# Where a mixer's adaptive-norm terms are summed, turned and loaded, on one core

## Chip, cores, metric

The kernel runs on one core of a Trainium2 chip. The metric is the time of one launch on the device in microseconds (us). Five engines matter: TensorE (PE; its weight loads are shown apart as PEld), VectorE (DVE), ScalarE (ACT), GpSimd (POOL), and SyncE (SP), whose queue issues nearly all loads from HBM.

## What is computed

Two layers of a trunk over 256 latent tokens and 256 context tokens, width 1024, all in float32. Each layer has three sublayers: a feed-forward block, a token mixer, a feed-forward block. Each sublayer's input is modulated and its output gated by terms computed from a conditioning vector (one for each of the two streams):

```python
mods_x = jnp.split((silu(c) @ ada_w[l] + ada_b[l])[:, None, :], 9, axis=-1)
x = ffn_sublayer(x, mods_x[0:3], ...)          # shift, scale, gate
y_x, y_c = token_mixer(modulate(x, sh_x, sc_x), modulate(ctx, sh_c, sc_c), ...)
# end of the mixer:
y_x = (sigmoid(g_ret)*y_ret + sigmoid(g_na)*y_na + sigmoid(g_fou)*y_fou) @ w_o
x = layer_norm(ALPHA * x + g_x * y_x, ln_w[l, 1], ln_b[l, 1])
x = ffn_sublayer(x, mods_x[6:9], ...)
```

In layer 1 the context stream ends with the keys and values of the mixer, so from there on only 256 tokens are left.

## The kernel before

**Sublayers.** `i` counts them from 0 to 5; the mixers are i = 1 (layer l = 0, both streams in the merge, N = 512 columns) and i = 4 (l = 1, one stream, N = 256). The order of every engine's work is written out by hand.

**Weights** come in units of 512 KB through a ring of 4 buffers: SP's `unit` (L389) loads `raw`, ACT's `rounded` (L517) writes the high part `wh`, DVE's `split` (L875) the low part `wl`, and PE multiplies three times for each pair of operands (`three`, L1360 to L1362). SP loads unit u when DVE has split unit u-4; ACT rounds unit u when PE has finished unit u-4. SP issues strictly in program order: a load that waits holds up all loads behind it.

**Adaptive-norm terms.** While a mixer or feed-forward block runs, DVE forms the sums for the next one (`ada`, L887 for the first term, L890 for the others): each step takes 128 rows of `ada_w` from one of only two buffers `araw` (SP's `ada_load`, L397) and adds them, scaled, to `acc`, one accumulator for each stream. The load of step n waits until step n-2 is done. A mixer has 24 steps: 8 for its own gate, 8 for the next shift (w = 0), 8 for the next scale (w = 1). Each finished sum is turned by eight 128x128 transposes into two PSUM banks (PE `mixer_turn`, L1421) and summed from there by DVE (`mixer_mods`, reduce L934, in bulk 1.2 us, and a small add L939). `acc` may be written again only after the turn.

**The merge** is the stage in question. Eight rounds `mm` = 0 to 7, each of five units: `v` (gate of branch 0), `v+1`, `v+2`, `v+3` (two half products), `v+4`; they use PSUM banks 0 to 5 (7 for the first product of all). After a round, DVE does `MERGE_PACE[mm]` steps of `ada`; between `v+3` and `v+4` of round mm, SP issues `MERGE_LOADS[mm]` loads. Ten steps are done ahead of the merge, 14 inside it. Before the change both layers share one pace, 2 2 2 0 3 3 2 0, and one table of loads, 0 2 2 2 2 3 2 1. In rounds 3 and 7 PE turns stream 0's sum between `v+2` and `v+3`, into banks 6 and 7; in layer 0 it turns stream 1's after `v+4` (into 2 and 3 for w = 1).

**The output projection** (`down`, matrix `w_o`) follows, in units q of its own: 8 in layer 1; 16 in layer 0, where the first 8 work on tiles 0 and 1 and the others on tiles 2 and 3. Its tiles take the banks `OUT_BANKS`: (6,7), (0,1), (2,3), (4,5) in layer 0, (6,7) and (0,1) in layer 1. Its moving operand is staged by ACT (L552) and DVE (L1029); the first four stages are done at the end of round 7, behind the rounding and splitting of that round's last unit. Before its first product PE also waits until stream 0's scale has been read out of banks 6 and 7 (`mod_taken`), and at q = 8 until the terms are ready (`mods_ready`).

Of the kernel before, what the change touches and what calls it, by code (L numbers as in the profile page):

```python
# [30 lines left out]
KD = D // P  # L31
# [86 lines left out]
def trunk(nc, io, out):  # L118
# [3 lines left out]
    with ctx:  # L122
# [140 lines left out]
        def both(i):  # L263

            return tiles(i) == NT
# [14 lines left out]

        def mod_bank(w, st):

            return 2 if w and st else 6

        def free_bank(i, n):

# [71 lines left out]
            return 1 + gate_halves(i) + 2 * sum(mod_sums(j) for j in range(i))  # L358

        MERGE_ADA = KD + 2  # L360
        MERGE_PACE = (2, 2, 2, 0, 3, 3, 2, 0)
        MERGE_LOADS = (0, 2, 2, 2, 2, 3, 2, 1)

        ada_ops = list(itertools.accumulate((chunk_streams(s, w) for i in range(-1, SUBS) for s, w in chunks(i) for _ in range(KD)),
                                            initial=0))
# [14 lines left out]
        def _(sp):  # L380
# [70 lines left out]
            def mixer(l):  # L451
                i = 3 * l + 1
                win = io["mix_w_in"][l]
                u = AT["ret_in", l]
                for n, (r, lo, hi) in enumerate(ret_steps(l)):
                    c0 = C_RG if r < KD else C_RK - KD * P if r < 12 else C_RQ - 12 * P
                    unit(u + n, rows(win, c0 + r * P, P))
                for k in range(KD):
                    unit(AT["rv", l] + k, rows(win, C_RV, D, k, k + 1))
                for j in range(4):  # L460
                    unit(AT["fu", l] + j, rows(win, C_FU + j * P, P))
                gate_bias(i)
                u = AT["na_in", l]
                for n in range(AR):
                    ada_load(i, n)
                for gi, c0 in enumerate((C_NK, C_NQ)):
                    for j in range(4):
                        unit(u + 4 * gi + j, rows(win, c0 + j * P, P))
                for j in range(4):
                    unit(AT["nv", l] + j, rows(win, C_NV, 512, 2 * j, 2 * j + 2))  # L470
                    if j:
                        ada_load(i, AR + j - 1)
                for n in range(AR + 3, MERGE_ADA):
                    ada_load(i, n)
                for h in range(4, NH):

                    sp.wait_ge(n_max, n0[l] + len(n_items[l]) // 4 * (h // 2 - 2) + 3 + h % 2)
                    load_bias(sp, l, h)
                u = AT["merge", l]
                for mm in range(KD):  # L480
                    c = mm * P
                    v = u + 5 * mm
                    unit(v, rows(win, c + C_GT, P))
                    unit(v + 1, rows(io["ret_w_out"][l], c, P))
                    unit(v + 2, rows(win, c + (C_GT + D), P))

                    unit(v + 3, rows(io["na_fou_w_out"][l], c, P))
                    for n in range(MERGE_LOADS[mm]):
                        ada_load(i, MERGE_ADA + sum(MERGE_LOADS[:mm]) + n)
                    unit(v + 4, rows(win, c + (C_GT + 2 * D), P))  # L490
                for q in range(KD * (2 if both(i) else 1)):
                    unit(AT["wo", l] + q, rows(io["mix_w_o"][l], 0, D, q % KD, q % KD + 1))
                    if q == KD - 2:
                        ln_params(i)
# [361 lines left out]
        def _(dve):  # L856
# [175 lines left out]
            def down(i, u, src, n):  # L1032

                for q in range(TAIL, n * (2 if both(i) else 1)):
                    split(u + q)
                    stage(i, src, n, q)
                    if both(i):
                        k0 = q - n
                        if k0 == 4:
                            residual(i + 1, 0)  # L1040
                        if k0 == (6 if n == KF else 5):
                            residual(i + 1, 1)
                        if k0 == (8 if n == KF else 6):
                            front(i + 1, 0)
                        if k0 == (10 if n == KF else 7):
                            front(i + 1, 1)
                        if k0 == 16:
                            rest(i + 1, 0)
                        if k0 == 18:
                            rest(i + 1, 1)  # L1050
# [164 lines left out]
            def mixer(l):  # L1215
# [74 lines left out]
                for mm in range(KD):  # L1290
                    v, q = u + 5 * mm, 5 + 40 * l + 5 * mm
                    z = rgz[:, mm, 0:N]

                    def gated(w, out, bank, uu):
                        dve.wait_ge(g_sig, 3 + 24 * l + 3 * mm + w + 1)
                        dve.wait_ge(unit_done, v + uu)
                        V.tensor_tensor(out, sg[:, w, 0:N], ps[:, bank, 0:N], ALU.mult).then_inc(g_sum, 1)

                    split(v + 4)
                    split(v + 5)  # L1300
                    gated(0, z, 1, 2)
                    split(v + 6)
                    split(v + 7)
                    for n, (w, bank) in enumerate(((1, 3), (2, 4))):
                        if n:
                            split(v + 8)
                            if mm == KD - 1:
                                for t in range(TAIL):
                                    stage(i, rgz, KD, t)
                        gated(w, sg[:, w, 0:N], bank, 4)  # L1310
                        dve.wait_ge(g_sum, q + 2 + 2 * n)
                        V.tensor_tensor(z, z, sg[:, w, 0:N], ALU.add).then_inc(g_sum, 1)
                        dve.wait_ge(g_sum, q + 3 + 2 * n)
                        if n == 0 and mm in (3, 7):
                            mixer_mods(i, mm // 4, 0)
                    if mm in (3, 7) and htiles(i + 1) == NT:
                        mixer_mods(i, mm // 4, 1)
                    for n in range(MERGE_PACE[mm]):
                        ada(i, MERGE_ADA + sum(MERGE_PACE[:mm]) + n)
                down(i, AT["wo", l], rgz, KD)  # L1320

            dve.sem_inc(ff_mul, 2)
# [32 lines left out]
        def _(pe):  # L1355
# [76 lines left out]
            def down(i, u, n):  # L1432
# [15 lines left out]

                if i % 3 == 1:
                    pe.wait_ge(g_sum, 5 + 40 * l + 5 * (KD - 1) + 1)  # L1450
                    pe.wait_ge(mod_taken, 4 * l + htiles(i + 1) // LT + 1)
                total = 2 * n if both(i) else n
                for q in range(total - TAIL):
                    half, k0 = divmod(q, n)
                    staged(q)
                    if q == n:
                        if i % 3 == 1:
                            pe.wait_ge(g_sum, 5 + 40 * (l + 1))
                            pe.wait_ge(mods_ready, 2 * (i + 2))
                        else:  # L1460
                            pe.wait_ge(ff_mul, 2 + ff0(i) + len(ffn_steps(i)))
                    if n == KF and half:
                        if k0 == 10:
                            turn(i + 1, 0)
                        if k0 == 12:
                            turn(i + 1, 1)
                    for t in range(LT * half, LT * half + LT):
                        ins = product(q, t, first=k0 == 0, last=k0 == n - 1)
                    ins.then_inc(unit_done, 1)
# [195 lines left out]
            def mixer(l):  # L1665
# [85 lines left out]
                for mm in range(KD):  # L1751
                    v, sgn, smn = u + 5 * mm, 24 * l + 3 * mm, 40 * l + 5 * mm

                    pe.wait_ge(g_sig, sgn + 1)
                    if mm:
                        form_a(v, 0, src, N)
                    pe.wait_ge(g_sum, smn + 1)
                    form_a(v + 1, 1, (oh, ol), N, src_at={0: (o_lo, 3 * l + 1), 4: (o_lo, 3 * l + 2), 6: (o_lo, 3 * l + 3)} if mm == 0 else {})
                    pe.wait_ge(g_sig, sgn + 2)
                    form_a(v + 2, 2, src, N)  # L1760
                    if mm in (3, 7):
                        mixer_turn(i, mm // 4, 0)
                    pe.wait_ge(g_sum, smn + 4)
                    if mm == 0:
                        pe.wait_ge(n_lo, 4 * (l + 1))
                    form_a(v + 3, 3, (ah, al), N, kts=4, last=False)
                    form_a(v + 3, 4, (fh, fl), N, kts=4, row=4)
                    pe.wait_ge(g_sig, sgn + 3)
                    form_a(v + 4, 5, src, N)
                    if mm in (3, 7) and htiles(i + 1) == NT:  # L1770
                        if mm == 7:
                            pe.wait_ge(g_sig, sgn + 5)
                            pe.wait_ge(g_sum, smn + 7)
                        mixer_turn(i, mm // 4, 1)
                down(i, AT["wo", l], KD)

            pe.wait_ge(c_silu, 1)
# [83 lines left out]
```

## Time and profile before

| | us |
|---|---|
| three runs | 2497.81, 2503.41, 2503.57; median 2503.41 |
| the profiled execution | 2500.18 |
| its span, first to last instruction | 2498.4 |
| busy PE / PEld / DVE / ACT / POOL | 2383.4 / 2080.4 / 1602.4 / 949.7 / 140.6 |

What is busy says little by itself: PE is, nearly always. What counts is where PE idles or runs at a lower clock, who releases it there, and what that engine had waited for in turn. In the rows below a line of a timeline reads: start, duration, engine, line of the kernel, operation, output tile <- inputs, shape, count, and in brackets the idle time before it with the releaser. SPq is SP's queue of DMA issues. A timeline merges equal neighbours: `x3` with 5.00 us is three issues with what lay between them.

### The profile page before, as it was taken

Reading aid. Unit: us, or ns where it says so; the run is one execution under the profiler, and the core shown is the slowest. Engines: PE = TensorE matmul, PEld = TensorE weight load, DVE = VectorE, ACT = ScalarE, POOL = GpSimd, SP = SyncE. Lnnn points to the kernel's source line nnn. Section 1 sums busy time; section 2 is a strip of 40 time slices with the busy share of each in tenths; the row PEclk is TensorE's granted clock in tenths of the full one; section 3 lists DMA queues with packets and bytes.
Section 4 is the critical chain, followed back from the end, with each engine's and each line's share of the span. In section 5 each row is a group of like instructions: output and inputs, shape, how many; then the busy total and the mean of one; then the engine's idle time right before and its main releaser. Section 6 shows DMA issues by size and latency. Waiting matters only on the chain.

```text
span 2498.4 us, 33234 instructions
## 1 busy us (share of the span) xinstructions
PE 2383.4 (95%) x13346; PEld 2080.4 (83%) x13346; DVE 1602.4 (64%) x2094; ACT 949.7 (38%) x1407; POOL 140.6 (6%) x171
## 2 busy tenths in 40 slices
PE   6999999999999999979999999999999999976997
PEld 6888988998877888778889898889888887975996
DVE  5566658856377446676666786666786647755655
ACT  2522345442136222353224463224564225333443
POOL 2000001101100000020000110000010110001000
PEclk8999999999999999989999999999999999987999
DMA  8445555652232425545456575456565334664763
GB/s 271 136 161 176 193 192 171 177 179 65 54 108 82 150 91 169 168 126 161 154 175 199 172 219 169 152 169 202 177 186 167 97 118 127 203 213 135 225 203 118
DMA packets 476669, 400.53 MB, mean 160 GB/s; under 512 B 36324, under 2 KB 428644, under 8 KB 476260
## 3 DMA queue, kind: packets, MB, share of 16 engines
q1 hardware_dynamic: 460640, 390.13, 49.2%
q10 hardware_dynamic: 15876, 8.28, 1.1%
q8 instruction: 106, 1.74, 0.3%
q14 instruction: 47, 0.39, 0.0%
HBM read 397.19 MB, written 1.17 MB: 159 GB/s over the span
## 4 chain that ended last, share of the span: by engine, by line
PE 84%; DVE 8%; ACT 3%; issue 2%; DMA 2%; ACTq 1%; POOL 0%; SPq 0%; POOLq 0%; DVEq 0%
PE ps L1360 25%; PE ps L1362 25%; PE ps L1361 25%; DVE wl L875 2%; PE ps L1571 1%; ACT wh L517 1%; ACT tB L535 1%; PE ps L1387 1%; PE ps L1649 1%; DVE st L943 1%; PE ps L1737 1%; PE ps L1628 1%; PE ps L1394 1%; DMA raw<-in_mix_w_in 1%; DVE nms L1185 1%
## 5 line engine op out<-in xcount | busy, mean ns | idle before, releaser
L875 DVE TENSOR_TENSOR wl<-raw,wh 128x1024 fp32r<-128x1024 f32 x576 | 701.6, 1221 | 651.9 <-ACT wh L517 650.5
L517 ACT ACTIVATE wh<-raw 128x1024 fp32r<-128x1024 f32 x576 | 609.1, 1059 | 1268.0 <-PE ps L1362 1166.0
L1360 PE MATMUL ps<-hh,wh 128*128 128x256 f32 (+1 forms) x2736 | 898.7, 328 | 44.3 <-DVE hl L976 19.8
L1361 PE MATMUL ps<-hl,wh 128*128 128x256 f32 (+1 forms) x2736 | 890.1, 325 | 0.0
L1362 PE MATMUL ps<-hh,wl 128*128 128x256 f32 (+1 forms) x2736 | 889.8, 325 | 0.0
L1360 PEld LDWEIGHTS ps<-hh,wh 128*128 128x128 f32 x2736 | 526.6, 192 | 90.5 <-issue 22.9
L1361 PEld LDWEIGHTS ps<-hl,wh 128*128 128x128 f32 x2736 | 526.5, 192 | 41.6 <-issue 1.0
L1362 PEld LDWEIGHTS ps<-hh,wl 128*128 128x128 f32 x2736 | 526.2, 192 | 40.6
L890 DVE SCALAR_TENSOR_TENSOR acc<-araw,c,acc 128x1024 f32<-128x1024 f32 x210 | 258.4, 1279 | 47.0 <-DMA araw<-in_ada_w 45.6
L1360 PE MATMUL ps<-wh,stage_h_f 128*128 128x512 f32 x616 | 240.8, 391 | 2.0 <-DVE stage_l_f L1029 2.0
L1362 PE MATMUL ps<-wh,stage_l_f 128*128 128x512 f32 x616 | 239.8, 389 | 0.0
L1361 PE MATMUL ps<-wl,stage_h_f 128*128 128x512 f32 x616 | 239.8, 389 | 0.0
L807 POOL TENSOR_SCALAR mv<-mv 128x1 f32<-128x1 f32 x42 | 41.5, 988 | 1868.5 <-DVE mv L945 1868.5
L1360 PEld LDWEIGHTS ps<-wh,stage_h_f 128*128 128x128 f32 x616 | 115.7, 188 | 27.6 <-DVE wl L875 4.3
L1362 PEld LDWEIGHTS ps<-wh,stage_l_f 128*128 128x128 f32 x616 | 115.6, 188 | 24.4
L1361 PEld LDWEIGHTS ps<-wl,stage_h_f 128*128 128x128 f32 x616 | 115.7, 188 | 23.7
L1360 PE MATMUL ps<-wh,hh 128*128 128x512 f32 x192 | 77.1, 402 | 2.4 <-DVE wl L875 2.2
L1361 PE MATMUL ps<-wl,hh 128*128 128x512 f32 x192 | 75.5, 393 | 0.0
L1362 PE MATMUL ps<-wh,hl 128*128 128x512 f32 x192 | 75.3, 392 | 0.0
L1029 DVE TENSOR_TENSOR stage_l_f<-g,stage_h_f 128x256 fp32r<-128x256 f32 x154 | 64.4, 418 | 0.0
L535 ACT ACTIVATE tB<-ps,modT 128x128 f32<-128x128 f32 x176 | 63.4, 465 | 1.1 <-PE ps L1429 1.1
L552 ACT ACTIVATE stage_h_f<-g 128x256 fp32r<-128x256 f32 x154 | 61.6, 400 | 0.0
(164 smaller groups left out, 2292.5 us busy)
## 6 DMA issues: line engine op xcount, KB each, us to landing
raw<-in_ffa_w SPq DMA_DIRECT2D x204, 512.0 KB, 3.8
raw<-in_ffb_w SPq DMA_DIRECT2D x168, 512.0 KB, 4.0
raw<-in_mix_w_in SPq DMA_DIRECT2D x148, 512.0 KB, 4.0
araw<-in_ada_w SPq DMA_DIRECT2D x136, 512.0 KB, 4.9
raw<-in_mix_w_o SPq DMA_DIRECT2D x24, 512.0 KB, 4.2
raw<-in_ret_w_out SPq DMA_DIRECT2D x16, 512.0 KB, 4.8
raw<-in_na_fou_w_out SPq DMA_DIRECT2D x16, 512.0 KB, 4.1
raw<-in_ada_w SPq DMA_DIRECT2D x8, 512.0 KB, 5.0
```

The lines of the kernel that those rows point to most:

```text
L517: A.activation(wh[:, s, :], raw[:, s, :], ACT.Copy).then_inc(w_rounded, 1)
L535: ins = A.activation(tB[:, t % 2, k * P:(k + 1) * P], y[:, k], ACT.Identity, scale=modT[:, i % 2, 1, k, s:s + 1], bias=modT[:, i % 2, 0, k ...
L552: A.activation(sh_[:, q % TAIL], src[:, k0, half * SEQ:(half + 1) * SEQ], ACT.Copy).then_inc(stage_hi, 1)
L807: link(G.tensor_scalar(m[:, 1:2], m[:, 1:2], EPS, None, ALU.add))
L875: V.tensor_tensor(wl[:, s, :], raw[:, s, :], f(wh[:, s, :]), ALU.subtract).then_inc(w_split, 1)
L890: ins = V.scalar_tensor_tensor(out=acc[:, st], in0=araw[:, m % AR], scalar=c, in1=acc[:, st], op0=ALU.mult, op1=ALU.add)
L943: ins = V.bn_stats(st[:, which, t % 2, 6 * k:6 * k + 6], src[:, k * 512:(k + 1) * 512])
L1029: V.tensor_tensor(sl_[:, q % TAIL], src[:, k0, half * SEQ:(half + 1) * SEQ], f(sh_[:, q % TAIL]), ALU.subtract).then_inc(stage_lo, 1)
L1185: link(V.tensor_reduce(nmax[:, t % 3, 0:1], y[:, 0:key_n(items[t])], AXX, ALU.max))
L1360: T.matmul(out, a[0], b[0], start=start, stop=False)
L1361: T.matmul(out, a[0], b[1], start=False, stop=False)
L1362: return T.matmul(out, a[1], b[0], start=False, stop=stop)
```

## The change

It has four parts, all in the two mixers. (1) `mod_bank`: the scale (w = 1) is turned into banks 2 and 3 for both streams, the shift into 6 and 7. (2) The turn of the scale's stream 0 moves from between `v+2` and `v+3` of round 7 to behind the last unit of the merge, with waits for the readers of banks 2 and 3; DVE sums it after its last `g_sum` addition, and PE's wait for `mod_taken` before the projection goes. (3) In layer 0, the turn of the scale's stream 1 moves from the end of the merge into the projection, before the products of q = 4; DVE sums it after its stage q = 6. (4) Layer 1 gets a pace and a table of loads of its own: pace 2 2 2 2 2 2 2 0, loads 0 2 2 2 2 2 2 2. Layer 0's stay.

```diff
         def mod_bank(w, st):
-            return 2 if w and st else 6
+            return 2 if w else 6
-        MERGE_PACE = (2, 2, 2, 0, 3, 3, 2, 0)
-        MERGE_LOADS = (0, 2, 2, 2, 2, 3, 2, 1)
+        MERGE_PACE = ((2, 2, 2, 0, 3, 3, 2, 0), (2, 2, 2, 2, 2, 2, 2, 0))
+        MERGE_LOADS = ((0, 2, 2, 2, 2, 3, 2, 1), (0, 2, 2, 2, 2, 2, 2, 2))
 # DVE, down
                     stage(i, src, n, q)
+                    if n == KD and both(i) and q == 6:
+                        mixer_mods(i, 1, 1)
 # DVE, merge
-                        if n == 0 and mm in (3, 7):
-                            mixer_mods(i, mm // 4, 0)
-                    if mm in (3, 7) and htiles(i + 1) == NT:
-                        mixer_mods(i, mm // 4, 1)
-                    for n in range(MERGE_PACE[mm]):
+                        if n == 0 and mm == 3:
+                            mixer_mods(i, 0, 0)
+                    if mm == 3 and htiles(i + 1) == NT:
+                        mixer_mods(i, 0, 1)
+                    if mm == 7:
+                        mixer_mods(i, 1, 0)
+                    for n in range(MERGE_PACE[l][mm]):
 # PE, down
                     pe.wait_ge(g_sum, 5 + 40 * l + 5 * (KD - 1) + 1)
-                    pe.wait_ge(mod_taken, 4 * l + htiles(i + 1) // LT + 1)
...
+                    if n == KD and both(i) and q == 4:
+                        mixer_turn(i, 1, 1)
 # PE, merge
-                    if mm in (3, 7):
-                        mixer_turn(i, mm // 4, 0)
+                    if mm == 3:
+                        mixer_turn(i, 0, 0)
...
-                    if mm in (3, 7) and htiles(i + 1) == NT:
-                        if mm == 7:
-                            pe.wait_ge(g_sig, sgn + 5)
-                            pe.wait_ge(g_sum, smn + 7)
-                        mixer_turn(i, mm // 4, 1)
+                    if mm == 3 and htiles(i + 1) == NT:
+                        mixer_turn(i, 0, 1)
+                pe.wait_ge(g_sig, 24 * l + 3 * (KD - 1) + 5)
+                pe.wait_ge(g_sum, 40 * l + 5 * (KD - 1) + 7)
+                mixer_turn(i, 1, 0)
                 down(i, AT["wo", l], KD)
```

## Rows read from the trace of the kernel before

**Rows 1.** The page's first part: busy time, share of the span, instructions.
```profile
PE 2383.4 (95%) x13346; PEld 2080.4 (83%) x13346; DVE 1602.4 (64%) x2094; ACT 949.7 (38%) x1407; POOL 140.6 (6%) x171
```

**Rows 2.** Busy time by stretch, layer 1's merge: length, engines, PEclk, DMA share, GB/s.
```profile
2130.00:2144.40 14.40, 14.40 (x123) 14.40 (x122) 10.37 (x13) 6.11 (x8) 0.00 (x0) 1.00 0.82 256
...
2174.00:2188.40 14.40, 14.40 (x122) 14.40 (x121) 8.29 (x12) 3.72 (x5) 0.00 (x0) 1.00 0.21 62
2188.40:2206.00 17.60, 11.44 (x77) 11.27 (x76) 7.92 (x9) 6.10 (x8) 0.00 (x0) 0.81 0.67 201
2206.00:2226.00 20.00, 15.68 (x115) 15.51 (x114) 10.80 (x13) 5.24 (x7) 0.00 (x0) 0.83 0.79 234
```

**Rows 3.** Timeline of PE, layer 1's merge: both turns and both stalls.
```profile
2159.50 1.04 PE L1421 MATMUL ps<-ident,acc 128*128 128x128 f32 x8
2160.29 0.36 PE L1360 MATMUL ps<-ah,wh 128*128 128x256 f32 x1
2160.49 0.28 PE L1361 MATMUL ps<-al,wh 128*128 128x256 f32 x1
...
2198.36 0.55 PE L1360 MATMUL ps<-hh,wh 128*128 128x256 f32 x1 [6.16 <-DVE wl L875]
...
2219.59 0.55 PE L1360 MATMUL ps<-hh,wh 128*128 128x256 f32 x1 [4.32 <-DVE wl L875]
...
2233.14 1.03 PE L1421 MATMUL ps<-ident,acc 128*128 128x128 f32 x8
```

**Rows 4.** Timeline of ACT, layer 1's merge: the rounding that ends the first stall.
```profile
2195.90 1.06 ACT L517 ACTIVATE wh<-raw 128x1024 fp32r<-128x1024 f32 x1 [13.79 <-DMA raw<-in_mix_w_in]
```

**Rows 5.** Timeline of SP's queue, layer 1's merge: when loads are issued.
```profile
2144.18 1.05 SPq L397 DMA_DIRECT2D araw<-in_ada_w  x2
...
2158.58 1.05 SPq L397 DMA_DIRECT2D araw<-in_ada_w  x2
...
2171.68 0.37 SPq L389 DMA_DIRECT2D raw<-in_na_fou_w_out  x1
2184.78 5.00 SPq L397 DMA_DIRECT2D araw<-in_ada_w  x3
```

**Rows 6.** Timeline of DVE, layer 1's merge: steps of the sums in rounds 2 and 4.
```profile
2154.33 2.67 DVE L890 SCALAR_TENSOR_TENSOR acc<-araw,c,acc 128x1024 f32<-128x1024 f32 x2
...
2184.00 0.75 DVE L887 TENSOR_SCALAR acc<-araw,c 128x1024 f32<-128x1024 f32 x1
```

**Rows 7.** Timelines of PE, ACT and DVE at the ends of both merges.
```profile
1019.46 1.03 PE L1421 MATMUL ps<-ident,acc 128*128 128x128 f32 x8
1022.52 0.73 PE L1360 MATMUL ps<-wh,stage_h_m 128*128 128x512 f32 x1 [2.02 <-DVE stage_l_m L1029]
...
2243.33 0.47 PE L1360 MATMUL ps<-wh,stage_h_m 128*128 128x512 f32 x1 [3.41 <-DVE stage_l_m L1029]
...
1019.72 1.06 ACT L517 ACTIVATE wh<-raw 128x1024 fp32r<-128x1024 f32 x1 [4.38 <-PE ps L1362]
...
2240.02 1.06 ACT L517 ACTIVATE wh<-raw 128x1024 fp32r<-128x1024 f32 x1 [1.81 <-PE ps L1362]
...
1020.81 1.22 DVE L875 TENSOR_TENSOR wl<-raw,wh 128x1024 fp32r<-128x1024 f32 x1 [1.63 <-ACT wh L517]
...
2240.29 1.22 DVE L934 TENSOR_REDUCE modT<-ps 128x8 f32<-128x1024 f32 x1
...
2241.63 1.22 DVE L875 TENSOR_TENSOR wl<-raw,wh 128x1024 fp32r<-128x1024 f32 x1
```

**Rows 8.** Busy time by stretch at both ends: columns as in rows 2.
```profile
2240.00:2250.00 10.00, 6.67 (x22) 5.37 (x23) 5.86 (x11) 3.91 (x8) 0.00 (x0) 0.83 0.51 153
1020.00:1030.00 10.00, 7.98 (x31) 6.30 (x30) 6.82 (x11) 3.90 (x9) 0.00 (x0) 0.83 0.40 124
```

**Rows 9.** Timelines of DVE and ACT, layer 0's projection: what surrounds the moved turn.
```profile
1024.74 1.22 DVE L934 TENSOR_REDUCE modT<-ps 128x8 f32<-128x1024 f32 x1
...
1035.39 1.06 ACT L517 ACTIVATE wh<-raw 128x1024 fp32r<-128x1024 f32 x1 [1.35 <-PE ps L1362]
...
1036.48 1.23 DVE L875 TENSOR_TENSOR wl<-raw,wh 128x1024 fp32r<-128x1024 f32 x1 [1.16 <-ACT wh L517]
```

More of the change, by code:

```diff
@@ L487, in mixer @@
                     unit(v + 3, rows(io["na_fou_w_out"][l], c, P))
-                    for n in range(MERGE_LOADS[mm]):
-                        ada_load(i, MERGE_ADA + sum(MERGE_LOADS[:mm]) + n)
+                    for n in range(MERGE_LOADS[l][mm]):
+                        ada_load(i, MERGE_ADA + sum(MERGE_LOADS[l][:mm]) + n)
                     unit(v + 4, rows(win, c + (C_GT + 2 * D), P))
@@ L1313, in mixer @@
                         dve.wait_ge(g_sum, q + 3 + 2 * n)
-                        if n == 0 and mm in (3, 7):
-                            mixer_mods(i, mm // 4, 0)
-                    if mm in (3, 7) and htiles(i + 1) == NT:
-                        mixer_mods(i, mm // 4, 1)
-                    for n in range(MERGE_PACE[mm]):
-                        ada(i, MERGE_ADA + sum(MERGE_PACE[:mm]) + n)
+                        if n == 0 and mm == 3:
[5 more added lines that the diff above has]
+                    for n in range(MERGE_PACE[l][mm]):
+                        ada(i, MERGE_ADA + sum(MERGE_PACE[l][:mm]) + n)
                 down(i, AT["wo", l], rgz, KD)
```

## The prediction

> **What bounds the kernel now.** I read the page's busy times first: PE is busy for 2383.4 of 2498.4 us [rows 1], so anything that keeps PE neither idle nor at a lower clock is free, and a change can win only in the 115 us of idle time and in the stretches of low clock beside them. The change touches the two merges and the projections behind them, so I cut these into stretches. In layer 0's merge PE has no idle time between rounds; each unit is 24 products of 512 columns there. In layer 1's it is at full load and full clock in rounds 1 to 4, and then 17.6 and 20.0 us long stretches show it busy for only 11.44 and 15.68 us, with a clock of 0.81 and 0.83 [rows 2]. So layer 1's rounds 5 and 6 hold most of what can be had.
>
> PE's timeline names the stalls: 6.16 and 4.32 us, both ended by a split of weights on DVE [rows 3]. The rest follows by asking each releaser what it had waited for. The split waited for ACT's rounding, and that had stood idle for 13.79 us for a load of `raw` [rows 4]. Was the transfer slow or late? SP's queue answers: its last weight issue ends at 2171.68 + 0.37 = 2172.05 and the next issue of anything is at 2184.78, 12.7 us later, and it is a load of `araw` [rows 5]. In the stretch of 2174 to 2188 the DMA engines move 62 GB/s, against 256 before [rows 2]: they had nothing to do. The `araw` load waited for the step two before it, number 16, and DVE ran that at 2184.00 to 2184.75 [rows 6], 0.03 us before the issue. Step 16 is the first of round 4, since round 3 has a pace of 0; the load that needs it is put in SP's round 5, which SP reaches a round ahead of DVE. The second stall is the same pattern one round later. Layer 0 has the same tables, but the four units in the ring are twice as long there, and PE does not see the pause.
>
> **Part 1, the new pace in layer 1.** It removes no work: 14 steps and 14 loads before and after. Step 16 moves to the end of round 3 and the three-step rounds are gone. The cost of the stall is read from the two turns on PE, which stand in the same place of rounds 3 and 7: 2233.14 - 2159.50 = 73.64 us [rows 3]. Four undisturbed rounds take 4 x 14.40, the pitch of the `araw` loads [rows 5] and the length of the stretch with PE at 14.40 [rows 2]: 57.60. The turn of round 3 lies between too. It is 0.79 us to the next product, and that product keeps 0.20 instead of 0.12 us to its follower [rows 3]: 0.87. So 73.64 - 57.60 - 0.87 = **15.2 us** are lost. Of these 6.16 + 4.32 = 10.5 are idle, and the other 4.7 are mainly the products at about half the clock behind each stall (it falls after 6.16 and 4.32 us without work).
>
> Does all of it go? What decides is which comes last before an `araw` load. With an even pace the two steps that a pair of loads needs stand at the end of DVE's round k, and SP reaches the pair (in its round k+2) only after its wait for the split that DVE does first in round k+1. By program order the steps are done by then. The rows of rounds 2 and 3 show it: steps until 2154.33 + 2.67 = 2157.00 [rows 6], loads at 2158.58 [rows 5], PE full. The new rounds 5 to 7 are this pattern again. I take 15.2; bounds: nothing, if another wait takes its place, and 15.2.
>
> What is late next in round 3: DVE now has its read-out (1.22 us for the reduce, and a small add) and two steps, 0.75 + 1.3, in one round, 3.5 us. Rounds 0 to 2 carried 2.67 and DVE was busy 10.37 of 14.40 [rows 2], so 4 us are free; and PE has three split units ahead of it, over 8 us of work. SP's weight issue moves by at most 2 us, where a unit is issued some seven units before PE takes it. I cost that at nothing. If the cover were gone, PE would idle by the 2 us.
>
> **Part 2, the end of layer 1's merge.** Now: PE's last product ends at 2243.33 - 3.41 = 2239.92; ACT rounds at 2240.02; the split could follow 1.09 us after the rounding's start, as it does in layer 0 (1019.72 to 1020.81), but starts 1.61 after it, at 2241.63, since DVE is still at the read-out (from 2240.29) [rows 7]. After: the read-out stands behind the last addition, which saves 1.61 - 1.09 = 0.52 us. The turn leaves the dense stream, where it cost 0.87, and fills 1.0 us of a gap that is 3.41 - 0.52 = 2.9 us long: the gap is set by ACT and DVE, so it does not grow. Sum **1.4 us**. The new waits for the readers of banks 2 and 3 are met: the addition they name is done before 2240.29 in this trace. PE's wait for `mod_taken` was not the last one; its removal is worth nothing.
>
> The clock after this gap is the one thing that I can only bound. Ten us around it show 0.83 in layer 1, with 3.41 us idle ahead, and also 0.83 in layer 0, where a turn and 2.02 idle us stand ahead [rows 8, 7]. The new gap of layer 1 looks like layer 0's old one, so I take no gain; if the clock held, it would be (1 - 0.83) x 10 = 1.7 us more.
>
> **Part 3, layer 0.** Here both turns were on PE: stream 0's in the dense stream of round 7, stream 1's at 1019.46, in the gap before the projection [rows 7]. After it, stream 0's is in the gap and stream 1's in the dense stream of the projection, at q = 4: minus 0.87, plus 0.87 (the same row of transposes; I bound it at 0.79 to 0.87 plus one fall of the clock, 1.7). The gap itself is set by ACT's rounding and DVE's split (1019.72, 1020.81), and the read-out was not in its way: DVE idled 1.63 us before that split [rows 7]. Sum **0**.
>
> Who queues behind the moved turn: all later products. It waits for stream 0's read-out. That is the reduce of 1024.74 [rows 9], done by 1026 and some 0.9 us earlier after the change; PE reaches q = 4 when ACT gets its release for the rounding of q = 7, at 1035.39 [rows 9]. That is 9 us of cover. DVE reads stream 1 out after stage 6, 1.4 us more; then the split of q = 7, now at 1036.48 [rows 9] (before that DVE idled 1.16), starts about 1 us later, and PE wants that unit at about 1035.3 + 3 x 2.7 = 1043.4 (a unit's pitch is ACT's 1.06 + 1.35 in that row and some 0.3 of staging). Each such round has over 1 us free, so DVE is level before its long work (residuals from q = 12) begins. PE's wait for `mods_ready` at q = 8 comes about 9 us after the terms are ready.
>
> A rule of the Trainium skill bears on the turns. Its page TensorE: Matmul & The Clock Gate, Part 4 (PE-mode transpose), says that a transpose does not count as work for the clock. What this trace has on it is mixed: behind a turn amid products the next ones come at full pitch [rows 3], and behind a turn with idle time the clock is low [rows 8]. By that rule the turn in the gap of layer 1 keeps nothing warm, which is what I take anyway.
>
> **The sum.** 15.2 + 1.4 + 0 = 16.6 us. Against the profiled execution: 2500.18 - 16.6 = 2483.6. That execution is 3.2 below the median of the three runs, 2503.41, and 2.4 above the lowest. The mean of all four is 2501.2, and I predict from that: 2501.2 - 16.6 = **2484.6 us**, 0.66% less. From the median it would be 2486.8.
>
> **Rivals.**
> (a) *Half the stall comes back.* DVE's fuller round 3, or an `araw` landing late for the new steps, moves one stall instead of removing it. Price: the smaller of the two, 4.32 idle and some 2.2 of low clock, 6.5 us: 2491. Against it: DVE's free 4 us. For it: the loads of rounds 5 to 7 now come without a pause.
> (b) *It doesn't remove it.* If transfers and not their issue were late, only part 2 would stay: 2501.2 - 1.4 = 2499.8. Against it: 12.7 us without any issue and 62 GB/s.
> (c) *A turn amid dense work lowers the clock.* One fall at q = 4 of layer 0 costs up to 1.7 us: 2486.3. The row against it: full pitch after 2160.49. It is the skill's rule above taken by its word.
> (d) *Slower.* Place: rounds 4 to 7 of layer 1. Seven transfers of 524 KB a round, 3.67 MB, now run through without the pause in which the queue drained. If they can't be kept up, PE waits for DMA in each round. It decides at the rate at which four rounds take 73.64 + 1.4 + 7.5 (0.3%) = 82.5 us, 20.6 each: 3.67 MB / 20.6 us = 178 GB/s. Below that it is slower: at 178, 2508.7. Against it: rounds 1 to 3 need 3.67 MB per 14.40 us = 255 GB/s, and the row has 256 with PE at full load [rows 2].
>
> **How the numbers follow.** Forecast 0.78; (a) 0.08; (b) 0.05; (c) 0.05; (d) 0.04. 0.3% is 7.5 us, about what a measurement of this kernel can tell from no change. Faster by more than that are the forecast, (c), and (a), whose 2491 is 10 below but with a spread of the runs of 3 us may fall short, so I give it three quarters: 0.78 + 0.05 + 0.06 = 0.89. Same: (b) and the rest of (a), 0.07. Slower 0.04. The range: below, the clock's 1.7 and the runs' scatter of 3.4 (2497.8 against 2501.2), with 2 for what changes in later clock falls: 2484.6 - 7 = 2477.5. Above: scatter of 2.3, (c)'s 1.7 and half of (a): 2493.
>
> **What would show it.** In the trace after: no gap in SP's issues over some 5 us in layer 1's merge; PE at 14.40 in every round with the clock at 1.00; from the turn of round 3 to the last product of the merge 4 x 14.40 us and the rest of a round; the split at the merge's end 1.1 us after the start of the rounding in both layers; the turn of layer 0 at q = 4 with no idle time before it and no slow products behind it. Wrong it would be if ACT still waited for `raw` in rounds 4 to 7, or if PE idled at q = 4 or q = 8 of layer 0's projection.

## The result, and the profile after

The changed kernel takes 2480.64 us in the median of six runs (2480.4 to 2483.76); the kernel before takes 2500.99 in six (2494.86 to 2503.57). The ratio, formed from all these runs and not from the two medians, is 0.9924, with a 95% interval of 0.9910 to 0.9938: 19 us, 0.76% less. The forecast was 2484.6, 16.6 us less. The profiled execution of the changed kernel took 2480.48 us with a span of 2478.6, against 2500.18 and 2498.4.

Where did the 19.8 us between the two spans go? I cut both at the same events of PE. From the turn of round 3 in layer 1 to the first product of that layer's projection it was 2243.33 - 2159.50 = 83.8 us [rows 3, 7] and is 2226.34 - 2159.00 = 67.3: **16.5 us** less. From that product to the start of the last one of the projection it was 23.25 and is 21.62: **1.6 us** less. The same two cuts in layer 0, from round 3's first turn to the projection's last product, give 180.3 and 180.1: **0.2 us**. The remaining 1.5 us lie outside these cuts, in code that the change does not touch (1.5 gained before layer 0's merge, 1.2 lost between the merges, 1.2 gained at the end); nothing here shows a cause for them.

First the merge of layer 1 by stretch (length, busy time of PE, PEld, DVE, ACT, POOL, then PEclk, DMA share, GB/s), which answers to rows 2:

```profile
2160.00:2220.00 60.00, 60.00 (x503) 60.00 (x502) 43.43 (x51) 25.07 (x34) 0.00 (x0) 1.00 0.80 256
2220.00:2230.00 10.00, 8.07 (x53) 7.13 (x52) 6.74 (x13) 4.21 (x8) 0.00 (x0) 1.00 0.48 154
```

PE is busy throughout at full clock, and the transfers run at 256 GB/s, the rate that rounds 1 and 2 had before. Even over the gap at the end the clock stays at 1.00. SP's queue in the same merge, to be read against rows 5:

```profile
2158.09 1.05 SPq L397 DMA_DIRECT2D araw<-in_ada_w  x2
...
2172.84 0.37 SPq L389 DMA_DIRECT2D raw<-in_na_fou_w_out  x1
2173.25 1.06 SPq L397 DMA_DIRECT2D araw<-in_ada_w  x2
2174.35 2.90 SPq L389 DMA_DIRECT2D raw<-in_mix_w_in  x2
...
2187.75 1.05 SPq L397 DMA_DIRECT2D araw<-in_ada_w  x2
...
2202.15 1.96 SPq L397 DMA_DIRECT2D araw<-in_ada_w  x2
```

Where 12.7 us passed without an issue, the pair of `araw` loads now follows the weight's issue within 0.1 us. DVE has the two steps that they need behind it, in the round that was empty:

```profile
2169.53 0.75 DVE L887 TENSOR_SCALAR acc<-araw,c 128x1024 f32<-128x1024 f32 x1
2170.39 1.28 DVE L890 SCALAR_TENSOR_TENSOR acc<-araw,c,acc 128x1024 f32<-128x1024 f32 x1
2171.59 2.37 DVE L875 TENSOR_TENSOR wl<-raw,wh 128x1024 fp32r<-128x1024 f32 x2
```

The steps end at 2171.67, and two splits follow back to back: DVE is late by no more than a split there, and PE, with units in hand, does not see it. The end of layer 1's merge, on PE, ACT and DVE, against rows 7:

```profile
2223.35 1.06 PE L1425 MATMUL ps<-ident,acc 128*128 128x128 f32 x8
2226.34 0.47 PE L1364 MATMUL ps<-wh,stage_h_m 128*128 128x512 f32 x1 [1.93 <-DVE stage_l_m L1029]
2226.65 0.39 PE L1365 MATMUL ps<-wl,stage_h_m 128*128 128x512 f32 x1
...
2223.48 1.06 ACT L517 ACTIVATE wh<-raw 128x1024 fp32r<-128x1024 f32 x1 [1.81 <-PE ps L1366]
...
2224.64 1.23 DVE L875 TENSOR_TENSOR wl<-raw,wh 128x1024 fp32r<-128x1024 f32 x1 [0.93 <-ACT wh L517]
```

The split starts 1.16 us after the rounding's start (it was 1.61), the idle time is 1.93 instead of 3.41, and the products behind it take 0.39 us, as in the dense stream. In layer 0, the turn in the gap, the first product, and the turn that moved into the projection:

```profile
1017.14 1.04 PE L1425 MATMUL ps<-ident,acc 128*128 128x128 f32 x8
1020.26 0.63 PE L1364 MATMUL ps<-wh,stage_h_m 128*128 128x512 f32 x1 [2.09 <-DVE stage_l_m L1029]
1020.69 0.63 PE L1365 MATMUL ps<-wl,stage_h_m 128*128 128x512 f32 x1
...
1032.88 1.03 PE L1425 MATMUL ps<-ident,acc 128*128 128x128 f32 x8
1033.67 0.47 PE L1364 MATMUL ps<-wh,stage_h_m 128*128 128x512 f32 x1
...
1033.95 1.23 DVE L934 TENSOR_REDUCE modT<-ps 128x8 f32<-128x1024 f32 x1 [0.89 <-PE ps L1425]
```

The idle time stays (2.09 against 2.02), the clock behind it is low (0.43 us from one product of 512 columns to the next, which is the level of 1.2 GHz), and the turn at q = 4 stands in the stream with no idle time before it and no slow products behind. Between its first transpose and the first product after it lie 0.79 us.

### The profile page after: what moved, and what is told of

Read it like the earlier page. It is cut to its first block, busy times and chain, and to the rows that moved or that the text cites. A ratio compares the mean times of both kernels' runs of the same rounds, so it can differ in the third digit from the quotient of the medians.

```text
span 2478.6 us, 33232 instructions
## 1 busy us (share of the span) xinstructions
PE 2377.6 (96%) x13346; PEld 2074.0 (84%) x13346; DVE 1604.0 (65%) x2094; ACT 949.6 (38%) x1407; POOL 140.7 (6%) x171
## 4 chain that ended last, share of the span: by engine, by line
PE 85%; DVE 8%; ACT 3%; issue 2%; DMA 1%; ACTq 1%; POOL 0%; SPq 0%; POOLq 0%; DVEq 0%
PE ps L1364 26%; PE ps L1365 25%; PE ps L1366 25%; DVE wl L875 2%; PE ps L1576 1%; ACT wh L517 1%; ACT tB L535 1%; PE ps L1391 1%; DVE st L943 1%; PE ps L1654 1%; PE ps L1742 1%; PE ps L1633 1%; PE ps L1398 1%; DVE nms L1187 1%; DMA araw<-in_ada_w 1%
## 5 line engine op out<-in xcount | busy, mean ns | idle before, releaser
L1364 PE MATMUL ps<-hh,wh 128*128 128x256 f32 (+1 forms) x2736 | 895.5, 327 | 31.6 <-DVE hl L976 19.8
```

Of the source, the lines that this page charges most:

```text
L1364: T.matmul(out, a[0], b[0], start=start, stop=False)
```

## The experiments

My theory: the gain is the pause of SP's queue (15.2 us) and the end of layer 1's merge (1.4), and layer 0 is neutral. The rivals were that the pace and the turns need one another, that only the empty round or only the bunched loads matter, and that layer 0's turn costs something. Single runs of one kernel spread over 3 to 12 us, so beside each ratio I give the cut from round 3's turn to the first product of the projection in layer 1 (**M**): 83.8 us before, 67.3 after. Where nothing stalls in it, this cut repeats to 0.02 us: the four traces with the changed kernel's code in layer 1 show 67.34 to 67.36, whatever layer 0 did.

### One half alone

The pace and loads of layer 1 alone, in the kernel before:

```diff
-        MERGE_PACE = (2, 2, 2, 0, 3, 3, 2, 0)
-        MERGE_LOADS = (0, 2, 2, 2, 2, 3, 2, 1)
+        MERGE_PACE = ((2, 2, 2, 0, 3, 3, 2, 0), (2, 2, 2, 2, 2, 2, 2, 0))
+        MERGE_LOADS = ((0, 2, 2, 2, 2, 3, 2, 1), (0, 2, 2, 2, 2, 2, 2, 2))
```

> The kernel before with only layer 1's new pace and table of loads; the turns, their banks and waits stay as before. My theory (the 16.5 us that the merge of layer 1 gained are 15.2 of pause in SP's queue and 1.4 at the merge's end): this one gains 15 us, ratio 0.9940, and its trace has PE at full clock from round 1 to round 7 of layer 1, while the gap behind the last unit of that merge stays at 3.4 us with a fall of the clock behind it. Rival (the pace alone only moves the stall; the moved read-out is needed too): some 8 us, ratio 0.997, and one stall is left in rounds 4 to 7.

Measured: 0.9936 (0.9921 to 0.9951), 2483.47 us. M is 68.66, 15.17 less than before, against the 15.2 that were forecast. Its merge and the first product of its projection:

```profile
2160.00:2222.00 62.00, 62.00 (x521) 62.00 (x520) 43.47 (x51) 25.80 (x34) 0.00 (x0) 1.00 0.81 254
...
2228.41 0.77 PE L1360 MATMUL ps<-wh,stage_h_m 128*128 128x512 f32 x1 [3.41 <-DVE stage_l_m L1029]
2228.97 0.63 PE L1361 MATMUL ps<-wl,stage_h_m 128*128 128x512 f32 x1
```

No stall is left, and the gap is the old one, with low clock behind it. The other half, the new turns with the old tables:

```diff
-        MERGE_PACE = ((2, 2, 2, 0, 3, 3, 2, 0), (2, 2, 2, 2, 2, 2, 2, 0))
-        MERGE_LOADS = ((0, 2, 2, 2, 2, 3, 2, 1), (0, 2, 2, 2, 2, 2, 2, 2))
+        MERGE_PACE = ((2, 2, 2, 0, 3, 3, 2, 0), (2, 2, 2, 0, 3, 3, 2, 0))
+        MERGE_LOADS = ((0, 2, 2, 2, 2, 3, 2, 1), (0, 2, 2, 2, 2, 3, 2, 1))
```

> The changed kernel with the old pace and loads in both layers; banks, turns and read-outs as changed. My theory: both stalls of layer 1's rounds 5 and 6 are back (6.2 and 4.3 us), the gap at the end of layer 1's merge is 2.9 us with the turn in it, and the gain is 1.4 us if the clock falls behind the gap and 3.0 if it holds: ratio 0.9994 to 0.9988. Rival (the turns are what costs time, by the clock or by their waits): a gain of 5 us or more, or a loss of 3 us or more.

Measured: 0.9989 (0.9978 to 0.9999), 2496.42 us. Both stalls are back:

```profile
2197.66 0.55 PE L1364 MATMUL ps<-hh,wh 128*128 128x256 f32 x1 [6.17 <-DVE wl L875]
...
2217.78 0.36 PE L1364 MATMUL ps<-hh,wh 128*128 128x256 f32 x1 [3.91 <-DVE wl L875]
```

M is 80.95, 2.9 less. Of this 1.3 is the end of the merge, the difference between the changed kernel and the one with the pace alone (68.66 - 67.34). The other 1.6 lie at the second stall, which was 0.4 us shorter and had no slow product behind it in this execution (0.36 us for the first one, where it was 0.55 [rows 3]); why is not shown, and one trace cannot tell it from chance. Read so, the two halves add up, and neither needs the other.

### Which table stops the queue

The loads as before, the pace new:

```diff
-        MERGE_LOADS = (..., (0, 2, 2, 2, 2, 2, 2, 2))
+        MERGE_LOADS = (..., (0, 2, 2, 2, 2, 3, 2, 1))
```

> The changed kernel, but layer 1 keeps its old table of loads (three in round 5) with the new pace. Theory (a load holds up the queue when SP reaches it a round before VectorE has done the step two before it): the third load of round 5 needs step 18, which VectorE does at the end of round 4, some 11 us after SP gets there; the same again in round 6. So both stalls stay, about as long as before: ratio 0.999, and SP's queue has pauses of about 10 us. Rival (only the empty round 3 of the pace matters): the stalls are gone, ratio 0.9924.

And the reverse, the loads new, the pace as before:

```diff
-        MERGE_PACE = (..., (2, 2, 2, 2, 2, 2, 2, 0))
+        MERGE_PACE = (..., (2, 2, 2, 0, 3, 3, 2, 0))
```

> The changed kernel, but layer 1 keeps its old pace (nothing in round 3, three steps in rounds 4 and 5) with the new table of loads. Theory: the first load of round 5 still needs step 16, now at the end of round 4, so the first stall stays whole (SP's queue pauses 12 us), and the ones after it too: ratio 0.999 or a little more. Rival (the three loads in one round are what stops the queue): the stalls are gone, ratio 0.9924.

Measured: 0.9961 (0.9947 to 0.9975) and 0.9969 (0.9955 to 0.9984); M is 72.1 and 75.8, so 4.8 and 8.4 us of the 15.2 are back. The pauses are there as expected, but I had the sizes wrong: I expected whole stalls and a ratio of 0.999, and they are smaller. SP's queue and the first stall of PE, of the pace-new kernel and then of the loads-new kernel:

```profile
2172.68 11.89 SPq L397 DMA_DIRECT2D araw<-in_ada_w  x3
2184.61 1.06 SPq L389 DMA_DIRECT2D raw<-in_mix_w_in  x2
...
2193.18 0.36 PE L1364 MATMUL ps<-hh,wh 128*128 128x256 f32 x1 [2.05 <-DVE wl L875]
```

```profile
2185.37 1.73 SPq L397 DMA_DIRECT2D araw<-in_ada_w  x2
2187.14 1.65 SPq L389 DMA_DIRECT2D raw<-in_mix_w_in  x2
...
2197.24 0.55 PE L1364 MATMUL ps<-hh,wh 128*128 128x256 f32 x1 [4.45 <-DVE wl L875]
```

The wait ends at about the same time in all three, when DVE does the awaited step of round 4. What differs is how many `araw` loads stand between its end and the next weights: three before (weights issued at 2189.82), two with the loads new, one with the pace new, where the other two had gone out ahead of the wait. PE's first stall is 6.16, 4.45 and 2.05 us long (the second one 4.32, 1.23 and 0.80). ACT's rounding, which ends the stall, comes 36.4, 34.7 and 32.3 us after round 3's turn, so with the same steps between them: 1.7 and 2.4 us for each load more. Not all of this is transfer. With three loads, the third waits once more, as the kernel before shows on DVE and on SP's queue:

```profile
2188.14 1.28 DVE L890 SCALAR_TENSOR_TENSOR acc<-araw,c,acc 128x1024 f32<-128x1024 f32 x1 [2.00 <-DMA araw<-in_ada_w]
...
2189.82 1.06 SPq L389 DMA_DIRECT2D raw<-in_mix_w_in  x2
```

The third step of the round needs the first of the three loads, and the third load needs that step: it goes out at 2189.45, as the step ends, and the weights right behind it. So PE loses what is left of the pause, plus what still leaves the queue ahead of the weights, once the ring has run dry. With a single load behind it, a pause of 10.5 us leaves PE idle for 2.05.

### The same pause on another queue

The kernel before, but the 14 loads of layer 1's merge are issued by GpSimd, with their waits and semaphores of their own:

```diff
+                    for n in range(MERGE_ADA, 24):
+                        ...
+                        pool.wait_ge(ada_step, ada_ops[m - AR + 1])
+                        G.dma_start(araw[:, m % AR, :], ...).then_inc(pool_loaded[m % AR], 16)
```

> The kernel before with its pace, turns and banks, but the 14 loads of the sums in layer 1's merge are issued from GpSimd's queue, each with the same wait for the step two before it; no weight load stands behind them. Theory (what hurts is only that the weights queue behind a waiting load): SP's queue has no pause, both stalls go though the steps stay where they were, and the kernel gains some 15 us, ratio 0.994. Rival 1 (VectorE's bunched steps, or the sums' data coming late, stop PE): the stalls stay, ratio 1.000. Rival 2 (the transfers from the other queue are slow enough to make VectorE wait in rounds 4 and 5 for more than the ring covers): one stall of a few us is left, ratio 0.997.

Measured: 0.9959 (0.9944 to 0.9975), M 72.1, 11.7 us less than before with the steps left where they were. The first stall is gone, and of the second 1.78 us are left. GpSimd's load and DVE's step, the same step one round later, SP's queue and PE:

```profile
2179.97 0.54 POOL L858 DMA_DIRECT2D araw<-in_ada_w  x1 [27.05 <-DVE acc L900]
2184.05 1.28 DVE L903 SCALAR_TENSOR_TENSOR acc<-araw,c,acc 128x1024 f32<-128x1024 f32 x1 [3.00 <-DMA araw<-in_ada_w]
...
2200.72 1.28 DVE L903 SCALAR_TENSOR_TENSOR acc<-araw,c,acc 128x1024 f32<-128x1024 f32 x1 [3.39 <-DMA araw<-in_ada_w]
...
2178.11 0.37 SPq L390 DMA_DIRECT2D raw<-in_mix_w_in  x1
2186.50 0.37 SPq L390 DMA_DIRECT2D raw<-in_na_fou_w_out  x1
...
2203.29 0.38 PE L1373 MATMUL ps<-hh,wh 128*128 128x256 f32 x1 [1.78 <-DVE wl L884]
```

This is rival 2 in its size, but not for the reason that it names. The load goes out only at 2179.97, because it needs a buffer that the first step of the same round gives free, and it lands 4.1 us later. In the kernel before, on SP's queue, the same step waited 2.00 us in the same way (the row of 2188.14 above), so the other queue makes at most 1 us of it. So the third step of the round waits 3.0 us for its data (3.39 in the next round), the splits queue behind it on DVE, and SP's next weight waits 8 us for a split. Against the pace-only kernel, which has the same turns, M is 3.5 us longer. So most of the 15.2 us was the weights standing behind a waiting load in one queue, and the bunched steps cost the other 3.5. The even pace removes both.

### Layer 0

Layer 0 with its old turns, banks and waits, layer 1 changed (two places of the edit against the changed kernel):

```diff
-            return 2 if w else 6
+            return 2 if w and (st or l) else 6
...
-                    if mm == 3:
-                        mixer_turn(i, 0, 0)
+                    if mm == 3 or mm == 7 and l == 0:
+                        mixer_turn(i, mm // 4, 0)
```

> The changed kernel, but layer 0 has its old turns, banks, read-outs and waits. My theory prices the moved turns of layer 0 at nothing (0.87 us out of round 7, 0.87 into the projection, the gap between unchanged): the same ratio as the changed kernel, 0.9924, within 0.5 us. Rival (the turn amid the projection, or its read-out at stage 6, costs something that the trace of one execution hides): this one is 1.5 us or more faster.

Measured: 0.9921 (0.9905 to 0.9938). To the first product layer 0 takes 125.47 us from round 3's first turn, against 124.66 with the change and 125.44 before: the 0.8 us that the change takes out of round 7 and puts back at q = 4. The ratios, each known to 4 us only, cannot rule out the rival's 1.5 us, but the traces can. The clock behind the gap held in this execution and fell in the changed kernel's first trace (see below), so the fair partner is the changed kernel's second trace, where it held too: from round 3's first turn to the last product of the projection it takes 177.7 us, and this kernel 177.5. Nothing of 1.5 us is hidden in the turns. The even pace in layer 0 too:

```diff
-        MERGE_PACE = ((2, 2, 2, 0, 3, 3, 2, 0), (2, 2, 2, 2, 2, 2, 2, 0))
-        MERGE_LOADS = ((0, 2, 2, 2, 2, 3, 2, 1), (0, 2, 2, 2, 2, 2, 2, 2))
+        MERGE_PACE = ((2, 2, 2, 2, 2, 2, 2, 0),) * 2
+        MERGE_LOADS = ((0, 2, 2, 2, 2, 2, 2, 2),) * 2
```

> The changed kernel with the even pace and table of loads in layer 0 too. Theory: layer 0's pause in SP's queue (15 us from 955 to 969 and one before it) goes, but PE never saw it, since four units of 5.44 us are in the ring; no gain, within 0.5 us of the changed kernel; ratio 0.9924. Rival (the pause costs something there too, or VectorE's round 3 with two read-outs and two steps for two streams, some 6.5 us, is too full): a difference of 2 us or more either way.

Measured: 0.9933 (0.9919 to 0.9947); from round 3 to the first product 124.65 us, to 0.01 the same as the changed kernel. SP's two pauses in layer 0 (24.6 and 14.8 us from one issue to the next in the kernel before) are gone, none above 8 us is left, and PE takes no notice: it has no idle time in layer 0's merge in either kernel. A unit lasts 5.44 us there, so four in the ring hold some 22 us of work.

### The gaps at the merges' ends

Layer 1's turn in the projection, so that its gap has no work of PE in it (DVE reads it out after stage 5):

```diff
+                    if n == KD and not both(i) and q == 2:
+                        mixer_turn(i, 1, 0)
...
-                mixer_turn(i, 1, 0)
+                if both(i):
+                    mixer_turn(i, 1, 0)
```

> The changed kernel, and layer 1's turn of the scale moves from the gap behind the merge into the projection, before the products of q = 2; VectorE reads it out after stage 5. So the gap of layer 1 is 2.9 us without any work of PE in it. Theory A (the clock held behind that gap because the time without products was 3.0 us and not 3.4): it holds here too, and the kernel is 0.9 us slower than the changed one. Theory B (it held because the turn filled a third of the gap): it falls, and the kernel is 0.9 + 1.6 = 2.5 us slower. Theory C (whether it holds is chance): the same trace in other runs of the same gap shows both.

Measured: 0.9943 (0.9925 to 0.9961). M is 67.35, so the gap is as long without the turn as with it (2.96 us idle), which shows that ACT and DVE set it. The clock fell behind it, and the projection took 24.16 instead of 21.62 us: 2.5 more, the sum of turn and fall. That is theory B's number, and it speaks against A, in one trace. Is it then the turn that holds the clock? I counted the first products of each projection in all 13 traces. Layer 1's gap with the turn and 1.93 us idle: the clock held in four, among them both traces of the changed kernel, and fell in three. With 3.41 us idle and no turn it fell in all three. Layer 0's gap, with a turn and 2.0 to 2.1 us idle: it fell in six and held in five, and the same kernel shows both. So a turn in the gap does not make sure that the clock holds, and theory C is right for such gaps; whether a gap of 3 us without a turn could hold too, one trace does not show. Here is the changed kernel in its second trace, at the place where the first shows 0.63:

```profile
1021.59 0.47 PE L1364 MATMUL ps<-wh,stage_h_m 128*128 128x512 f32 x1 [2.09 <-DVE stage_l_m L1029]
1021.90 0.40 PE L1365 MATMUL ps<-wl,stage_h_m 128*128 128x512 f32 x1
```

> The changed kernel once more, beside the next one, for a second sample of its trace. Expected: ratio to before 0.9924 within 0.0015; layer 1 from the turn of round 3 to the first product of the projection 67.3 us, layer 0 124.7 us as in every trace of this pace so far. Open is the clock behind the gaps: if it is chance, layer 1's gap (held here the first time) may show seven or eight slow products and then the kernel is 1.6 us longer; if the gap's make-up decides, it holds again.

Measured: 0.9931 (0.9918 to 0.9944), 2481.12 us; M 67.35; layer 0 to the first product 124.62. With a turn and 2 us idle, a fall that costs 1.6 us came in 9 of 18 gaps; with 3.4 us idle in three of three. In layer 0 this second trace is 2.4 us shorter than the first up to the projection's last product (177.7 against 180.1): 1.6 of it is the fall behind the gap, the rest mainly fewer slow products late in the projection.

If the gap is set by the rounding and the split of a unit that the first product does not need, its four stages can stand ahead of them:

```diff
-                    rounded(v + 8)
                     if mm == KD - 1:
                         act.wait_ge(unit_done, v + 4)
                         for q in range(TAIL):
                             stage(i, AT["wo", l], rgz, KD, q)
+                    rounded(v + 8)
# DVE
-                            split(v + 8)
                             if mm == KD - 1:
                                 for t in range(TAIL):
                                     stage(i, rgz, KD, t)
+                            split(v + 8)
```

> The changed kernel, and in round 7 the first four stages stand ahead of the rounding (ScalarE) and the split (VectorE) of that round's last unit, instead of behind them. Theory (the gap before the projection is ScalarE's rounding, then VectorE's split, then the first stage, none of which the first product needs but the stage): PE passes from the turn to the first product without idle time in both layers. That saves 2.1 us idle and 1.6 of low clock in layer 0 and 1.9 idle in layer 1: 5.6 us below the changed kernel, ratio to before 0.990. Rival (something else gates the first product, the weights' split or the sum of branch 2): the gap stays above 1 us and the ratio at 0.992.

Measured: 0.9917 (0.9902 to 0.9932), 2479.06 us; M 65.32. The ratio alone does not tell it from the changed kernel, and the 5.6 us that I expected are not there. I ran it again beside that one:

> The kernel with the stages ahead of the last rounding, once more, beside the changed kernel on one chip. Its first trace lost the gaps: 2.4 us in layer 0 and 2.0 in layer 1, and there is no fall of the clock at either. Expected here the same, and a ratio to before about 0.0020 below that of the changed kernel in the same rounds; if the gain was luck of one trace, the ratios are the same and a gap is back.

Measured: 0.9904 (0.9891 to 0.9918), 2475.22 us, against 0.9931 and 2481.12 for the changed kernel measured beside it (the slowest of these runs, 2476.9, is below the fastest of those, 2479.96); M again 65.32. PE at the end of layer 0's merge:

```profile
1018.36 1.04 PE L1425 MATMUL ps<-ident,acc 128*128 128x128 f32 x8
1019.16 0.47 PE L1364 MATMUL ps<-wh,stage_h_m 128*128 128x512 f32 x1
1019.47 0.39 PE L1365 MATMUL ps<-wl,stage_h_m 128*128 128x512 f32 x1
```

The turn passes into the first product without idle time and the clock is full, in both layers and both traces. To the first product it saves 2.3 us in layer 0 and 2.0 in layer 1, and a fall of 1.6 wherever there would have been one. In layer 0 part of that is lost again: to the last product of the projection it is 176.6 and 176.4 us, against 177.7 for the changed kernel with the clock held. A later gap, where DVE is busy with the residual, grew from 2.6 to 3.7 and 3.2 us and has more slow products behind it. It is the fastest kernel of the study, 20 us below the one before in the first measurement and 25 in the second.

## Why the prediction was right

**Part 1, the stalls: right in mechanism and size.** 15.2 us were forecast and 15.17 measured with the pace alone. The order that I argued from the program holds in the trace: steps until 2171.67, loads at 2173.25. The fuller round 3, costed at nothing, cost nothing. Rivals (a), (b) and (d) are out: no stall came back, all of it went, and the queue carried 256 GB/s without a pause.

**Part 2, the end of layer 1's merge: right, 1.3 us against 1.4.** Of the clock behind the gap I took no gain, because the new gap looked like layer 0's old one, and I named 1.7 us as the other end. In the measured trace it held, for 1.6 us. The term that was short is this one, and that it held there was luck. What the runs put in its place is a frequency: this gap held in four of seven traces. Some 0.9 us (4/7 of 1.6) would have been the better entry.

**Part 3, layer 0: right at zero.** Round 3 to the first product is 0.8 us shorter, and the turn at q = 4 takes 0.79 us to the next product, as the text put it. With the clock held behind the gap, the old and the new turns of layer 0 are 0.2 us apart to the projection's last product. Rival (c), a fall of the clock at the turn amid products, did not come: the product behind the turn took 0.47 us and the ones after it 0.40. The covers of 9 us for `mod_taken` and `mods_ready` held, since PE never waited at q = 4 or q = 8.

**The sum.** Forecast 16.6; the traces give 16.5 in the merge and 1.6 of clock, 18.1. The other 1.7 of the 19.8 us between the two spans are the 0.2 of layer 0 and 1.5 outside the changed code, which no part of the forecast accounts for. The ratio's interval reaches from 15.5 to 22.5 us and holds 16.6 as well as 18.1; the second measurement of the same kernel gave 0.9931, 17 us. One sum of the range does not come out: 2484.6 with the scatter of 2.3, the 1.7 of (c) and half of (a)'s 6.5 is 2491.9 and not 2493; nothing else hangs on it.

**The rule of the skill.** The Trainium skill (TensorE: Matmul & The Clock Gate, Part 4) says that a transpose does not count as busy time for the clock in the way that a matmul does. The runs do not contradict it, but they do not show it either. A turn amid products lowered nothing, and the gap with a turn in it held the clock about as often as not, but it also has less idle time than the gap of 3.4 us that never did.

## What to carry to other kernels

Where loads of two kinds share an in-order queue, a load that waits for a later consumer stops the other kind too. Compare the round in which the queue reaches each load with the round in which the awaited step is done, and place the step ahead by program order, not by time. The price for the compute engine is the pause minus what the ring holds, plus what still leaves the queue ahead of the starved kind, plus the slow products behind a longer stall. Moving the waiting loads to another engine's queue took away 11.7 of the 15.2 us here, the even pace all of them. And look at what stands ahead of the first item of the next stage on each helper engine: work that is needed only three items later may stand there.

## What the runs showed of the hardware that I had not expected

- The granted clock behind a turn and about 2 us of idle time is not fixed by the program: in layer 0 the same kernel with the same idle time (2.09 us) had it low in one execution (0.63 us for a product of 512 columns) and full in another (0.40). A fall costs 1.6 us in layer 1's projection (23.25 against 21.63). How much of the spread of the runs it makes is not shown: the changed kernel's two traces are 2.4 us apart in layer 0 and 0.6 us in their spans.
- A second and a third `araw` load of 512 KB ahead of starved weights put off the rounding that ends PE's stall by 2.4 and 1.7 us, though the queue issues two in 1.05 us when nothing holds it up. For the third, part of this is its own wait for a step.
